# Expert gate and up products on one Trainium2 core: rounded-part matmuls first, then remainder matmuls, in place of turn and turn about

## The reference

```python
def expert_choice_moe(x, w_router, w_gate, w_up, w_down):
    ...
    aff = jax.nn.softmax(jnp.matmul(xt, w_router).astype(jnp.float32), axis=-1)
    gate, idx = lax.top_k(aff.T, cap)
    xg = xt[idx]
    h = jax.nn.silu(jnp.einsum('ecd,edf->ecf', xg, w_gate)) * jnp.einsum('ecd,edf->ecf', xg, w_up)
    y = jnp.einsum('ecf,efd->ecd', h, w_down) * gate[..., None].astype(x.dtype)
    out = jnp.zeros_like(xt).at[idx.reshape(-1)].add(y.reshape(-1, D))
```

## Time and profile before

| | |
|---|---|
| median of 3 runs | 1766.36 us (1766.05 to 1768.7) |
| profiled execution | 1767.66 us, of which the span from first to last instruction is 1765.8 us |
| mean granted TensorE clock | 0.988 of full speed |
| TensorE matmuls busy | 1717.8 us, 97% of the span |
| TensorE weight loads busy | 1554.8 us, 88% |
| VectorE busy | 1192.7 us, 68% |
| ScalarE busy | 1074.2 us, 61% |
| GpSimd busy | 391.2 us, 22% |

### The profile page before, as it was taken

One profiled execution on the slowest core, in us unless ns is written; L12 is line 12 of the kernel. 1 busy time (PEld: TensorE's weight loads), 2 busy tenths in 40 slices (PEclk: granted clock), 3 DMA queues, 4 the chain that ended last, 5 costly groups with the idle time before them and its releaser, 6 DMA issues.

```text
span 1765.8 us, 30625 instructions
## 1 busy us (share of the span) xinstructions
PE 1717.8 (97%) x10812; PEld 1554.8 (88%) x10812; DVE 1192.7 (68%) x2367; ACT 1074.2 (61%) x2140; POOL 391.2 (22%) x552
## 2 busy tenths in 40 slices
PE   9999999899999989998999999999999999999994
PEld 9789898788888878887999999999999999999994
DVE  4442533488888972147777877787777877778776
ACT  4333333389999983332566756667666666666665
POOL 1322402255555542220110011100110011100112
PEclk9999999899999999998999999999999999999998
DMA  7556645665545742334786787867868678676885
GB/s 237 129 164 196 193 127 152 161 168 156 150 150 145 217 114 107 114 114 166 266 269 247 256 263 237 273 237 256 273 227 274 240 263 279 220 265 251 268 274 220
DMA packets 203488, 367.18 MB, mean 208 GB/s; under 512 B 39055, under 2 KB 64655, under 8 KB 202831
## 3 DMA queue, kind: packets, MB, share of 16 engines
q1 hardware_dynamic: 190268, 320.92, 54.3%
q0 software_dynamic: 13120, 44.96, 9.9%
HBM read 321.67 MB, written 50.45 MB: 211 GB/s over the span
## 4 chain that ended last, share of the span: by engine, by line
PE 48%; DVE 2%; DMA 2%; ACT 1%; POOL 1%; issue 0%; DVEq 0%; SPq 0%; ACTq 0%; POOLq 0%
PE psum L2148 21%; PE psum L2150 10%; PE psum L2167 3%; PE psum L2168 3%; PE psum L2169 3%; PE psum L2170 3%; PE psum L2171 3%; PE psum L2133 1%; DMA own_rows<-x 1%; DMA x<-y_s,index 0%; DVE raw_weights L1848 0%; DMA rows_s<-xn,tokens 0%; DVE weight_parts L1781 0%; ACT xT_e L2012 0%; POOL final_stats L1740 0%
## 5 line engine op out<-in xcount | busy, mean ns | idle before, releaser
L2148 PE MATMUL psum<-x_parts,weight_parts 128*128 128x384 f32 x2048 | 583.6, 359 | 0.0
L2150 PE MATMUL psum<-x_parts,weight_parts 128*128 128x192 f32 x2048 | 512.7, 250 | 0.0
L1781 DVE TENSOR_TENSOR weight_parts<-raw_weights,weight_parts 128x1024 fp32r<-128x1024 f32 x384 | 451.4, 1220 | 69.3 <-ACT weight_parts L1980 69.3
L1980 ACT ACTIVATE weight_parts<-raw_weights 128x1024 fp32r<-128x1024 f32 x384 | 381.8, 1055 | 23.5 <-DMA raw_weights<-in_w_gate 11.0
L2150 PEld LDWEIGHTS psum<-x_parts,weight_parts 128*128 128x128 f32 x2048 | 391.2, 191 | 0.6
L2148 PEld LDWEIGHTS psum<-x_parts,weight_parts 128*128 128x128 f32 x2048 | 384.4, 188 | 0.8
L603 PE MATMUL psum<-x_hi,w_parts 128*128 128x512 f32 x624 | 193.6, 390 | 0.0
L1721 POOL DMA_INDIRECT x<-y_p,index x15 | 24.1, 1609 | 640.4 <-DVE y_s L1843 640.4
L2007 ACT ACTIVATE h_parts<-up_sum 128x192 fp32r<-128x192 f32 x128 | 46.7, 365 | 169.8 <-DVE up_sum L1796 169.6
L1212 PE MATMUL psum<-w_o_parts,mixed_parts 128*128 128x512 f32 x576 | 140.8, 397 | 1.2 <-DVE w_o_parts L1349 1.2
L603 PEld LDWEIGHTS psum<-x_hi,w_parts 128*128 128x128 f32 x624 | 117.1, 188 | 26.9 <-issue 2.6
(11 more groups left out here) (221 smaller groups left out, 3127.9 us busy)
## 6 DMA issues: line engine op xcount, KB each, us to landing
raw_weights<-in_w_gate SPq DMA_DIRECT2D x32, 2048.0 KB, 7.8
raw_weights<-in_w_up SPq DMA_DIRECT2D x32, 2048.0 KB, 8.6
raw_weights<-in_w_down SPq DMA_DIRECT2D x32, 2048.0 KB, 8.9
mixed<-in_w_in SPq DMA_DIRECT2D x96, 256.0 KB, 4.3
q_parts<-q SPq DMA_DIRECT2D x188, 128.0 KB, 3.1
bias_da<-da_rows SPq DMA_DIRECT2D x31, 512.0 KB, 4.4
q<-mixed POOLq DMA_DIRECT2D x96, 128.0 KB, 3.1
mixed<-in_x SPq DMA_DIRECT2D x12, 512.0 KB, 6.9
```

What stands on the lines that cost most here:

```text
L1781: dve.tensor_tensor(part_half(u, 1, half), src, part_half(u, 0, half).bitcast(F32), ALU.subtract).then_inc(split, 1)
L1980: act.activation(part_half(u, 0, half), src, ACT.Copy).then_inc(rounded, 1)
L2148: pe.matmul(out.rearrange("p (h n) -> p h n", h=2), w[:, 0, k, cols], x_parts[:, k, :, :], start=(k == 0), stop=False)
L2150: mm = pe.matmul(out[:, 0:SLOTS], w[:, 1, k, cols], x_parts[:, k, 0, :], start=False, stop=(k == KT - 1))
```

## The change

In `product` the loop over k is cut into two loops. The eight wide matmuls come first, then the eight narrow ones. Nothing else differs; the semaphore increment stays on the last narrow matmul of the up product.

```diff
@@ -2147,6 +2147,7 @@
                             pe.wait_ge(x_split, second_half)
                         pe.matmul(out.rearrange("p (h n) -> p h n", h=2), w[:, 0, k, cols], x_parts[:, k, :, :],
                                   start=(k == 0), stop=False)
+                    for k in range(KT):
                         mm = pe.matmul(out[:, 0:SLOTS], w[:, 1, k, cols], x_parts[:, k, 0, :],
                                        start=False, stop=(k == KT - 1))
                     return mm
```

## The result

| | before | after |
|---|---|---|
| median of 15 runs | 1767.85 us (1765.46 to 1769.78) | 1772.63 us (1769.98 to 1776.37) |
| ratio | | 1.0029, 95% interval 1.0022 to 1.0035 |
| span of the profiled execution | 1765.8 us | 1769.9 us |

The change makes the kernel slower by 0.29%, about 5 us: inside the range of 1761 to 1774, but above what was called no change, and some three times the forecast loss of 1.7 us. Of the 4.5 us between 1768.1 and the measured 1772.63, 1.5 lie in the kernel before, whose median over 15 runs is 1767.85 where three runs had given 1766.36; the other 3 us are what the change costs beyond the forecast.

What follows compares the result with a forecast made beforehand. TensorE, busy throughout the experts' products, was taken to bound the kernel. Pairs longer by 0.0010 us on 240 products add 1.7 us to the median 1766.36, the other steps nothing: 1768.1 us, range 1761 to 1774.

Steps and rivals of the forecast that it cites:

- Step 1: Products: a wide matmul follows a wide one in 7 of 8 places; slot becomes 0.1733 us, bounds 0.17 to 0.176.
- Step 2: Products: a narrow matmul follows a narrow one in 7 of 8 places; the load sets 0.112 us, bounds 0.108 to 0.120.
- Step 3: Wide-narrow pair 0.2853 us from 0.2843, +0.0010; 7 pairs in 240 products of experts 0 to 14: +1.7 us.
- Step 4: Stage's first product: the wait for the second half of x, reached after 4 wide matmuls, hides by 0.1 us; costs nothing.
- Step 5: ScalarE and VectorE's round of moves, sums, weight splits: 4.593 us a slice against TensorE's 4.549; hides losses, takes most of gains.
- A: The forecast itself: product slots as in rows of equal matmuls; 1768.1 us, spread 1764 to 1772.6; chance 0.68.
- B: Loads in products keep the 0.108 us pace inside a pair; pair 0.2813, capped -3.7 us, 1762.7; chance 0.15.
- C: Loads run ahead in narrow rows, only columns count: narrow slot 0.093, pair 0.2666; capped -10.4 us, 1756; chance 0.05.
- D: Narrow rows' 192 columns with an exposed load cost 0.120, like 256; pair 0.2933, +15.1 us, 1781.5; chance 0.08.
- E: Start marks in products are true: wide matmuls in a row 0.197, narrow 0.112; +41 us, 1808; chance 0.04.

## Why the prediction was right or wrong

**What bounds.** Right: TensorE stays busy for the whole stretch, and its longer products are the time. By the nanosecond marks an expert's products grew from 36.386 to 36.683 us, and 14 x 0.297 = 4.2 us of the stretch's 4.46 are the slots; 0.3 lies in the stretches between products, 0.23 of it in the transposes, and isn't explained by an experiment.

**Step 1, the wide slot: the step that failed.** The prediction took 0.1733 for seven of a row's eight and left the eighth as before. Settled slots are that, but a row pays 0.0067 + 0.0025 + 0.0084 = 0.0176 us more at its start, where the forecast had 0.0028 (the eighth at 0.1761). The bound given, 0.176 a slot, took it in: 0.1755 was measured as a mean. That was luck in part, since the bound came from a doubt about two rounded marks and not from a slow start; and by the prediction's own sign (wrong if the spacing leaves 0.17 to 0.176) single slots of 0.180 and 0.182 are outside. The error was to take a price from rows that had long settled. The trace of before had rows that hadn't: the pair at 480.73 is the second slot of a row of four, whose slots are 257, 171, 175 and 178 ns, and a 512-wide row that starts at 41.31 us has 233, 236, 228, 233 and 231 ns before its 226.7.

**Step 2, the narrow slot.** Right. The load sets it, 0.1117 in a row; the mean of a row with its first at 0.108 is 0.111, which is 0.003 us a product less than the forecast. That 128, 160 and 192 columns give the same loads' slots in rows shows it.

**Step 3, the sum.** The mechanism was right and its size wrong: a product +0.0185 us in place of +0.0070, by 240 on the path: +4.4 in place of +1.7 us. The slots behind each expert's first product close the account: +0.0063 by the forecast's slots unrounded, +0.0148 for the wide row's start, -0.003 for the narrow row, 0.0181 in sum, and 0.0180 was measured (2275.35 to 2293.33 ns). The prediction's own sign, products of 36.4 to 36.6 us an expert, was missed: they took 36.69. The measured medians differ by 4.8, the two profiled executions by 4.1. The last expert was off the path as said: its down product still starts 0.57 us after line 1803. What it waits for there includes the transfer shown above, which the prediction did not name.

**Step 4, the first product.** The forecast was that the wait would hide by 0.1 us. It does not quite: the loads run ahead of the matmuls, and the load for block 4 waited for line 1826. The products of expert 0 grew by 0.35 us, those of the others by 0.30. From its first product to that of expert 1, though, it takes 909.87 - 854.00 = 55.87 us, 0.30 more than the 55.57 of before, so nothing of it reached the time.

```profile
854.93 0.64 PEld L2148 LDWEIGHTS psum<-x_parts,weight_parts 128*128 128x128 f32 x4 [0.28 <-DVE x_parts L1826]
```

**Step 5, the circle.** Right as far as it was used: 4.59 us a slice, hidden, and a loss counted in full. That it caps a gain was argued and has not been tried, since no kernel run here had faster products by more than 0.02 us an expert.

**The rivals.** A comes nearest, with 4.8 of the +6.2 us at the upper end of its own range. B's 0.108 exists, for one load between long neighbours, but not in a row. C, loads at the pace of transposes, did not occur: the disagreement of the trace with the 81 ns of the Trainium skill (TensorE: Matmul & The Clock Gate, "Back-to-back issue gap") holds in the 14 places of a slice where a narrow matmul follows a narrow one, 109 to 117 ns each. For 128 columns, the width of that figure, the run with rows of 128-wide matmuls has 110 to 113 ns in these places. D asked for 0.120 and got 0.111 as a mean. E, the marks as they stand, is ruled out by 173.3 in settled rows; the first wide slot still shows 201.7 by the matmuls' marks where the loads say 180.

**The chances.** Slower by over 0.2% had 0.23, and it is what happened; one outcome can't say that this was too low. The range held because the wide slot's upper bound was carried into it.

## What to carry to other kernels

Sorting matmuls by kind gained nothing here, as it took no load away: a matmul shorter than its successor's weight load cost that load, 0.108 to 0.112 us, in every order tried, and a change of width could start a series of slower slots. (An order that does save a load was not tried.) For a short row of wide matmuls a slot price from a long settled row is too low on average; take the first slots of rows of that length too. Where the bound engine is as close to the others' circle as here (4.549 and 4.593 us a slice), count a loss on it in full and a gain only up to the slack; of these two the loss was measured and the gain was not.

## What the runs showed of the hardware

- Slots in settled rows with a weight load each, at full clock: 0.120 us for 256 columns, 0.1733 for 384, 0.2267 for 512; that is a steady 0.0133 over the columns at 2.4 GHz (0.1067, 0.160 and 0.2133). By the same sum 224 columns would ask 0.1067 and 240 ask 0.1133; the load takes over between them, at 0.108 alone and 0.1117 in a row.
- A pair of one wide matmul and one exposed load has two prices in turn, 0.2843 and 0.2867, and the width of the narrow one chooses: 160 and 192 the lower, 128, 208 and 224 the upper. Fewer columns can be slower, and more columns too, though the load covers both. The kernel before has the lower price.
- A row of four or more 384-wide matmuls settled at 0.1733 after three slots (128 or 192 columns in the narrow row before it) or six (160 columns, or 512-wide matmuls before it), each time with 0.176 and 0.182 as the last two; slots of up to 0.185 stand in the longer series. Rows of two end before they settle. Behind a row of its own width nothing has to settle. What chooses the entry, and why 160 and 192 avoid most of it in turn, stays open.
- No kernel run here was faster than the one before.
